# Gate products of u computed in the convolution stage, while u is on chip, and a merge stage without them

## The reference

```python
u = _rmsnorm(h, w['g_mix'][i])
proj = u @ w['w_in'][i]
...
xbc = silu(depthwise conv of width 3 over the tokens of xbc, plus conv_b)
...
gates = jax.nn.sigmoid(u @ w['w_gate'][i] + w['b_gate'][i])
g_a, g_s = jnp.split(gates, 2, axis=-1)
merged = g_a * (att @ w['w_att_up'][i]) + g_s * (ssm @ w['w_ssm_up'][i])
h = h + merged @ w['w_out'][i]
```

## Time and profile before

| | |
|---|---|
| three runs before | 3404.81, 3406.62, 3408.55 us, median 3406.62 |
| the profiled execution, its own time | 3404.74 us |
| its span, first to last instruction | 3403.2 us |
| TensorE busy | 2773.6 us, 81% |
| VectorE busy | 1692.1 us, 50% |
| ScalarE busy | 1264.1 us, 37% |
| GpSimd busy | 288.6 us, 8% |
| mean granted TensorE clock | 0.908 |

### The profile page before, as it was taken

One profiled execution on the slowest core, in us unless ns is written; L12 is line 12 of the kernel. 1 busy time (PEld: TensorE's weight loads), 2 busy tenths in 40 slices (PEclk: granted clock), 3 DMA queues, 4 the chain that ended last, 5 costly groups with the idle time before them and its releaser, 6 DMA issues. The chain is left out here.

```text
span 3403.2 us, 43260 instructions
## 1 busy us (share of the span) xinstructions
PE 2773.6 (81%) x15560; PEld 2377.3 (70%) x15560; DVE 1692.1 (50%) x2153; ACT 1264.1 (37%) x1737; POOL 288.6 (8%) x328
## 2 busy tenths in 40 slices
PE   3999999337754992698989695489999999999597
PEld 2898887236541771586868584489999999998475
DVE  5000000557877774333333224767777777777324
ACT  4111111346645554222222111055555555555222
POOL 0000000100020001000000000001111111110121
PEclk9999999578987995899999797589999999999799
DMA  8412211652113336546463562178787878785312
GB/s 263 111 62 93 81 63 56 183 156 61 33 55 88 103 108 187 175 123 197 127 194 93 169 195 74 33 228 258 235 258 235 260 235 257 240 258 168 115 39 97
DMA packets 477377, 507.50 MB, mean 149 GB/s; under 512 B 21096, under 2 KB 434664, under 8 KB 476424
## 3 DMA queue, kind: packets, MB, share of 16 engines
q1 hardware_dynamic: 444032, 375.44, 36.8%
q0 software_dynamic: 33264, 130.98, 12.1%
HBM read 397.12 MB, written 109.25 MB: 149 GB/s over the span
## 5 line engine op out<-in xcount | busy, mean ns | idle before, releaser
L1790 DVE TENSOR_TENSOR ex_w_lo<-ex_w_raw,ex_w_hi 128x2048 fp32r<-128x2048 f32 x195 | 443.8, 2291 | 142.9 <-ACT ex_w_hi L1747 142.9
L1879 PE MATMUL ex_ps_u<-ex_x,ex_w_hi 128*128 128x384 f32 x2048 | 411.5, 341 | 5.1 <-DVE ex_w_lo L1790 5.1
L1747 ACT ACTIVATE ex_w_hi<-ex_w_raw 128x2048 fp32r<-128x2048 f32 x195 | 370.5, 1909 | 0.8
L1879 PEld LDWEIGHTS ex_ps_u<-ex_x,ex_w_hi 128*128 128x128 f32 x2048 | 349.1, 189 | 6.2 <-issue 5.5
L1879 PEld LDWEIGHTS ex_ps_u<-ex_x,ex_w_lo 128*128 128x128 f32 x2048 | 265.6, 191 | 0.6
L1898 PE MATMUL ex_ps_d<-ex_w_hi,ex_h 128*128 128x512 f32 x768 | 265.8, 400 | 0.0
L1879 PE MATMUL ex_ps_u<-ex_x,ex_w_lo 128*128 128x192 f32 x2048 | 265.5, 272 | 0.0
L354 DVE TENSOR_TENSOR w_lo<-w_raw,w_hi 128x2048 fp32r<-128x2048 f32 x15 | 34.3, 2290 | 403.3 <-ACT w_hi L322 403.3
L328 ACT ACTIVATE stage<-ps 128x512 f32<-128x512 f32 (+1 forms) x102 | 55.8, 547 | 413.9 <-PE ps L376 358.4
L1898 PE MATMUL ex_ps_d<-ex_w_lo,ex_h 128*128 128x512 f32 x512 | 202.8, 396 | 0.0
L1898 PEld LDWEIGHTS ex_ps_d<-ex_w_hi,ex_h 128*128 128x128 f32 x768 | 144.6, 188 | 35.0
(11 more groups left out here) (366 smaller groups left out, 5219.4 us busy)
## 6 DMA issues: line engine op xcount, KB each, us to landing
ex_w_raw<-in_w_exp_gate SPq DMA_DIRECT2D x64, 1024.0 KB, 5.3
ex_w_raw<-in_w_exp_up SPq DMA_DIRECT2D x64, 1024.0 KB, 6.7
ex_w_raw<-in_w_exp_down SPq DMA_DIRECT2D x64, 1024.0 KB, 6.9
mg_w_raw<-in_w_gate SPq DMA_DIRECT2D x48, 512.0 KB, 5.2
w_raw<-in_w_in SPq DMA_DIRECT2D x15, 1024.0 KB, 5.6
mg_w_raw<-in_w_ssm_up SPq DMA_DIRECT2D x24, 512.0 KB, 6.1
xbcT_d<-stage POOLq DMA_DIRECT2D x5, 1536.0 KB, 5.6
cv_raw<-xbcT_d POOLq DMA_DIRECT2D x10, 768.0 KB, 5.6
```

Source lines behind the costliest of these rows:

```text
L1747: act.activation(w_hi[:, j % CUT], w_raw[:, j % RAW], ACT.Copy).then_inc(w_hi_done, 1)
L1790: dve.tensor_tensor(w_lo[:, j % CUT], w_raw[:, j % RAW], w_hi[:, j % CUT].bitcast(F32), ALU.subtract).then_inc(w_split, 1)
L1879: last = pe.matmul(ps_u[:, j % 2, m, 0:wide * C], w[:, s, k, cols], x[:, k, 0:wide].rearrange("p a c -> p (a c)"), start=i == 0, stop=i == ...
```

## The change

The 1152 gate matmuls (16 column tiles of w_gate by three blocks by 24) leave `merge_branches` and come into `convolve`, which now runs while u_hi and u_lo are still in SBUF. There they are 48 gate units, tile by tile. In each of the ten turns TensorE does one gate unit and then the turn's 12 transposes; 38 units follow behind the last turn. w_gate is loaded and split once (16 tiles of 128 x 1024), where the merge did it once for each block. ScalarE copies each gate product from PSUM (`gst`), SyncE stores it in DRAM (`g_d`).

`merge_branches` is written anew with 36 matmuls per unit: it loads the gate products from `g_d` (L1278 of the changed kernel), opens the gates ahead of the products, keeps o for all tokens in SBUF, holds y in two buffers and splits y of the next block a piece at a time between units (`TURNS`), and has four slots of PSUM for the products where it had two. In both stages the hardware loops (`Fori`) are gone: the instructions stand one behind the other. The core of the diff:

```diff
+    UNITS = [(i, col, blk) for i, col in enumerate(gate_tiles) for blk in range(NB)]
+    NG, NTL = len(UNITS), len(gate_tiles)
+    STEPS = max(XT, NG)
...
+            for n in range(XT):
+                if n >= 2:
+                    pool.wait_ge(mixed, n - 1)
+                pool.dma_start(raw[:, n % 2], xbcT_d[n]).then_inc(landed[n % 2], 16)
+                pool.dma_start(taps[:, n % 2], taps_d[n]).then_inc(landed[n % 2], 16)
...
+            conv(0)
+            split_lo(0)
+            for n in range(1, XT):
+                conv(n)
+                if n % NB == NB - 1:
+                    split_lo(n // NB + 1)
+            for t in range(XT // NB + 1, NTL):
+                split_lo(t)
...
+            def split_hi(t):
+                act.wait_ge(w_landed[t % 2], 16 * (t // 2 + 1))
+                if t >= 2:
+                    act.wait_ge(g_full, NB * (t - 1))
+                act.activation(w_hi[:, t % 2], w_raw[:, t % 2], ACT.Copy).then_inc(w_hi_done, 1)
...
+                if n < NG:
+                    act.wait_ge(g_full, n + 1)
+                    if n >= 2:
+                        act.wait_ge(g_out[s], 16 * (n // 2))
+                    act.activation(gst[:, s], ps_g[:, s], ACT.Copy).then_inc(g_copied, 1)
+                    if n % NB == 0 and n // NB + 1 < NTL:
+                        split_hi(n // NB + 1)
...
+            for n in range(STEPS):
+                s = n % 2
+                if n < NG:
+                    i, _, blk = UNITS[n]
+                    toks = slice(blk * BLK, (blk + 1) * BLK)
+                    pe.wait_ge(w_hi_done, i + 1)
+                    if n >= 2:
+                        pe.wait_ge(g_copied, n - 1)
+                    terms = [(w, u, k) for w, u in ((w_hi, u_hi), (w_hi, u_lo), (w_lo, u_hi)) for k in range(KT)]
+                    for j, (w, u, k) in enumerate(terms):
+                        if j == 2 * KT:
+                            pe.wait_ge(w_split, i + 1)
+                        last = pe.matmul(ps_g[:, s], w[:, i % 2, k], u[:, k, toks], start=j == 0, stop=j == len(terms) - 1)
+                    last.then_inc(g_full, 1)
+                if n < XT:
+                    pe.wait_ge(silu_done, n + 1)
+                    if n >= 2:
+                        pe.wait_ge(copied, n - 1)
...
+            def load_w(t):
+                if t >= 2:
+                    sp.wait_ge(w_split, t - 1)
+                col = gate_tiles[t] * P
+                sp.dma_start(w_raw[:, t % 2], w_view[:, :, col:col + P]).then_inc(w_landed[t % 2], 16)
+
+            for t in range(2):
+                load_w(t)
+            for n in range(STEPS):
+                s = n % 2
+                if n < NG:
+                    i, col, blk = UNITS[n]
+                    if blk == 0 and i + 2 < NTL:
+                        load_w(i + 2)
+                    sp.wait_ge(g_copied, n + 1)
+                    sp.dma_start(g_d[col // KT, col % KT, blk], gst[:, s]).then_inc(g_out[s], 16)
+                if n < XT:
+                    sp.wait_ge(copied, n + 1)
+                    sp.dma_start(xb_out[:, :, n * P:(n + 1) * P], nat[:, s]).then_inc(nat_out[s], 16)
...
-    parts = ((w_gate, 0, KT, "u"), (w_gate, D, KT, "u"), (w_att_up, 0, KO, "o"), (w_ssm_up, 0, KT, "y"))
-    KW = 3 * KT + KO
-    starts = (0, KT, 2 * KT, 2 * KT + KO)
+    KW = KO + KT
     M = D // P
+    UNITS = [(blk, tile) for blk in range(NB) for tile in range(M)]
+    NU = len(UNITS)
+    SLOTS = 4
+    TURNS = {2: (0, 1), 3: (2,), 4: (3,), 5: (4,), 6: (5,), 7: (6, 7)}
...
+            for n, (blk, tile) in enumerate(UNITS):
+                s = n % 2
+                cols = slice(tile * P, (tile + 1) * P)
+                if n >= 2:
+                    sp.wait_ge(w_split, n - 1)
+                for w, k0, k1 in ((w_att_up, 0, KO), (w_ssm_up, KO, KW)):
+                    sp.dma_start(w_raw[:, s, k0:k1], w.rearrange("(k p) c -> p k c", p=P)[:, :, cols]).then_inc(w_landed[s], 16)
+                if n >= 2:
+                    sp.wait_ge(gated, n - 1)
+                sp.dma_start(g_raw[:, s], g_d[:, tile, blk].rearrange("j p t -> p j t")).then_inc(g_landed[s], 16)
...
+            load_o(0)
             pool.wait_ge(newton, 4)
             load_y(0)
-            for blk in range(NB):
-                with pool.Fori(0, M // 2 - 1) as it:
-                    for s in range(2):
-                        store(blk, it, s, pool.snap(2 * it + s))
-                        seen_stored(blk, it, s)
-                store(blk, M // 2 - 1, 0, M - 2)
-                seen_stored(blk, M // 2 - 1, 0)
-                if blk < NB - 1:
-                    for name, hi_src, lo_src in sources:
-                        load(name, blk + 1, hi_src, lo_src)
+            for blk in range(1, NB):
+                load_o(blk)
+            for n, (blk, tile) in enumerate(UNITS):
+                s = n % 2
+                if tile == 0 and blk + 1 < NB:
+                    pool.wait_ge(y_lo_done, KT * (blk + 1))
                     load_y(blk + 1)
...
+            for n, (blk, tile) in enumerate(UNITS):
+                open_gates(n)
+                if n + 1 < NU:
+                    split_hi(n + 1)
+                if n:
+                    round_sum(n - 1)
+                if blk + 1 < NB:
+                    for k in TURNS.get(tile, ()):
+                        turn_y(blk + 1, k)
+            round_sum(NU - 1)
...
+            def combine(n):
+                s = n % 2
+                dve.wait_ge(full, n + 1)
+                dve.wait_ge(scaled, n + 1)
+                if n >= 2:
+                    dve.wait_ge(lo_done, n - 1)
+                for j in range(2):
+                    dve.tensor_tensor(prods[:, s, j], ps[:, n % SLOTS, j], gates[:, s, j], ALU.mult).then_inc(multiplied, 1)
+                dve.wait_ge(multiplied, 2 * n + 2)
+                dve.tensor_tensor(prods[:, s, 0], prods[:, s, 0], prods[:, s, 1], ALU.add).then_inc(summed, 1)
...
+                pe.wait_ge(w_hi_done, n + 1)
+                if n >= SLOTS:
+                    pe.wait_ge(multiplied, 2 * (n - SLOTS + 1))
+                if tile == 0:
+                    pe.wait_ge(o_landed[blk], 32)
+                terms = [(w, v, k) for w, v in ((w_hi, o_hi), (w_hi, o_lo), (w_lo, o_hi)) for k in range(KO)]
+                for i, (w, v, k) in enumerate(terms):
+                    if i == 2 * KO:
+                        pe.wait_ge(w_split, n + 1)
+                    pe.matmul(ps[:, n % SLOTS, 0], w[:, s, k], v[:, k, toks], start=i == 0, stop=i == len(terms) - 1)
+                terms = [(w, v, k) for w, v in ((w_hi, y_hi), (w_lo, y_hi), (w_hi, y_lo)) for k in range(KT)]
+                for i, (w, v, k) in enumerate(terms):
+                    if tile == 0 and i < KT:
+                        pe.wait_ge(y_hi_done, KT * blk + i + 1)
+                    if tile == 0 and i >= 2 * KT:
+                        pe.wait_ge(y_lo_done, KT * blk + i - 2 * KT + 1)
+                    last = pe.matmul(ps[:, n % SLOTS, 1], w[:, s, KO + k], v[:, blk % 2, k], start=i == 0, stop=i == len(terms) - 1)
+                last.then_inc(full, 1)
...
-    convolve(nc, tiles(xbcT), taps, ident, xb, bcT)
+        convolve(nc, u_hi_now, u_lo_now, w_gate, list(range(2 * KT)), tiles(xbcT), taps, ident, xb, bcT, g)
```

More of the change, by code:

```diff
@@ L1216, in _ @@
         @block.gpsimd
         def _(pool):
-            def load(name, blk, whole, half):
-                if blk:
-                    pool.wait_ge(used[name], blk)
-                for part, src, landed in zip(acts[name], (whole, half), a_landed[name]):
-                    pool.dma_start(part[:].bitcast(F32), src[:, :, blk * BLK:(blk + 1) * BLK]).then_inc(landed, 16)
-            def store(blk, it, s, tile):
-                n = it * 2 + (M * blk + s)
-                pool.wait_ge(lo_done, START + n + 1)
-                pool.sem_inc(pass_pool, 1)
-                for src, out in ((mh, m_hi_d), (ml, m_lo_d)):
-                    pool.dma_start(out[:, bass.ds(tile, 1), blk * BLK:(blk + 1) * BLK].rearrange("p o t -> p (o t)"), src[:, s].bitcast(F32)).then_inc(out_done[s], 16)
@@ new lines, in _ @@
+            for n, (blk, tile) in enumerate(UNITS):
+                s = n % 2
+                if tile == 0 and blk + 1 < NB:
+                    pool.wait_ge(y_lo_done, KT * (blk + 1))
+                    load_y(blk + 1)
+                pool.wait_ge(lo_done, n + 1)
+                for src, out in ((mh, m_hi_d), (ml, m_lo_d)):
+                    pool.dma_start(out[:, tile, blk * BLK:(blk + 1) * BLK], src[:, s].bitcast(F32)).then_inc(out_done[s], 16)
+            for done in out_done:
+                pool.wait_ge(done, 32 * NU // 2)
@@ new lines, in turn_y, with open_gates @@
+            def turn_y(blk, k):
+                act.wait_ge(y_landed, 16 * (blk + 1))
+                if blk >= 2:
+                    act.wait_ge(full, M * (blk - 1))
```

(43 more changed lines are left out.)

252 lines of the change are left out of this document (89 added, 163 removed).

## The result

| | before | after |
|---|---|---|
| median | 3405.72 us (3403.69 to 3408.55, 4 runs) | 3308.33 us (3306.51 to 3311.64, 4 runs) |
| ratio of after to before | | 0.9715, 95% interval 0.9698 to 0.9731 |
| span of the profiled execution | 3403.2 us | 3304.9 us |
| mean granted clock | 0.908 | 0.911 |

What follows compares the result with a forecast made beforehand. TensorE was taken to bound the merge and to be nearly free in the convolution. Merge -304.4 and convolution +216.4 give -88.0; 3404.74 - 88.0 + 1.9 = 3319 us, range 3303 to 3354 (the forecast's own 3308 to 3331).

Steps and rivals of the forecast that it cites:

- The frame: Whole change: 1152 matmuls move from the TensorE-bound merge to the convolution, where TensorE is nearly free; -304.4 and +216.4 us.
- Nine turns, 7.6 us each: Convolution, turns after the first: 7.6 us each from slower load landings, between 6.9 and 9.5; 68.4 us in all.
- 178 us under 188: Merge, steady units: 178 us of transfers hidden under 188 us of matmuls, the closest cover of the change.
- 38 units at 24 x 0.2266: Convolution, gate units behind the turns: 5.44 us each at the old merge's matmul pace, 206.7 us in all.
- Hidden, by 1 us: Convolution, first turn: low part of the weights ready at 616.0, before TensorE asks at 617.3, so no wait.
- End of the convolution, 7.7: Convolution, after the last gate unit: last copy 0.9 us, then store, landing and barrier 6.8 us.
- Merge's start, 43.8: Merge, stage start to end of first unit: 43.8 us, as that unit can't end before y arrives.
- Tail, 11.4: Merge, end of the stage: 13.4 us less a pair of sigmoids and one product done ahead, so 11.4 us.
- Block changes: Merge, between blocks: with o whole in SBUF and y split between units, the 38.6 us of losses go, except the cold start.
- Transfers as the limit, in turns or units: Two rivals, 12% each: transfers set convolution turns of 9.5 us (+17, 3336 us) or merge units of 9.5 us (+31, 3350).
- Waiting for the own stores: Rival, 3%: convolution gate units wait for their `gst` stores; at a landing of 15 us, +97, 3416 us.
- The clock: Rival, 4%: TensorE's clock stays low in the convolution's turns, making them 12.6 us; +45, 3364 us.

## Why the prediction was right, by its own steps

**The frame held.** Matmuls moved from a stage that TensorE bounds to one with TensorE nearly free; -304.4 + 216.4 was forecast and -308.9 + 212.8 came. That the total came out within 10 us is in part luck, as the next two steps show.

**Nine turns, 7.6 us each: mis-sized, 6.91.** The step is "a fuller queue makes landings longer: at 9 us it is 7.7". The rows have the loads of `cv_raw` landing in 5.5 us at a share of 0.88, no longer than the 6.4 of the earlier trace rows, and TensorE has no pause in the turns, so its own work is the turn: 24 x 0.2333 + 1.23 = 6.83. That the units there cost next to nothing was the mechanism, and the experiment with the units behind the turns shows it. The same step made too much of the transfers in the merge: 178 us under 188 were worked out with 277 and 322 GB/s. From 1600 to 1780 us in after the two queues moved 28.14 MB in 51.2% of 180 us and 15.40 MB in 21.8%, 305 and 392 GB/s while at work; the share was 0.72, not above 0.75, and even with double stores at 0.90 nothing waited. The 2 us of loss were 0.

**38 units at 24 x 0.2266: too low, 5.60.** The pace was taken from a stage whose weight tiles lie on multiples of 64 bytes, and these don't. This is 6.2 us of the sum, in the opposite direction to the turns; the two errors hid each other. The tile list of the change shows the odd start; nothing in the trace of before puts a price on it.

**"Hidden, by 1 us": wrong.** Counted from the stage's start, the low part was ready at 14.5 us, where 12.4 were forecast (616.0 - 603.64): the taps began 8.17 us in (611.21), not 6.15. TensorE asked at 11.6 us and not at 13.7: its first matmul came 1.2 us sooner, and it was at full pace after eight matmuls and not sixteen. That made 2.91 us of wait; the first turn was 1.5 us longer than forecast, and moving the split gave back those 1.5.

**End of the convolution, 7.7: 3.8.** It was read from the merge's end, where two stores follow one another on GpSimd's queue; here one store follows on SyncE's, 2.0 us to landing in the page's row for all 48:

```profile
g_d<-cv_gst SPq DMA_DIRECT2D x48, 256.0 KB, 2.0
```

**Merge's start, 43.8: 39.7.** The load of y took 9.05 us to its first rounding (10 forecast) but was issued 20.0 us into the stage, not 20.8, and the eight low-by-high matmuls at its end ran at full clock. **Tail, 11.4: 13.0.** From the last store's issue (1790.01) to the next stage are 8.6 us, where the earlier trace rows have 6.8; why that landing is slower wasn't tried.

**Block changes.** That the 35.6 us go (38.6 of losses less the 3.0 of the cold start) was right. The prediction put it down to o being whole and y being split between units; in this merge the runs say 30.3 for the late loads, y's early load among them, and 1.7 for the pieces of y.

**The rivals.** Transfers as the limit, in turns or units: the two rows at shares of 0.88 and 0.90 with TensorE busy throughout speak against both. Waiting for the own stores: `gst` is waited for by nobody, stores land in 2.0 to 3.4 us. The clock: 1.00 in the turns. The Trainium skill, TensorE: Matmul & The Clock Gate, Part 4, says that transposes don't count as busy for the clock. Where they stand alone (the units behind the turns) the clock is 0.55, and the trace agrees so far; but TensorE is idle for half of that stretch (25.5 of 56 us busy), which may be reason enough, and no run separates the two. Between gate units the transposes cost nothing, so the rule doesn't price this change.

## What to carry to other kernels

Work that an idle engine can take inside another stage's chain is nearly free until its own time per turn passes the chain's: here ten units of 5.6 us added 0.8 each. Behind that point every unit costs its full length, so the pace must be taken for the new place, with the tiles where they will lie: a 32-byte tile ahead of the weights cost 7 us, and moving it cost nothing. At a stage's start ask for what the first units need and hold the rest: an earlier first unit was worth nothing until the later loads (4.2 MB of o, and the variance) no longer stood beside the next weights. The moved tile, the first split ahead of the taps and the held start together give 3291.29 us, 17 below the changed kernel.

## What the runs showed of the hardware that wasn't expected

- fp32r matmuls of 128 x 128 by 128 x 512 at a clock of 1.00 take 0.2267 us with weight tiles at multiples of 64 bytes, and 0.2333 with tiles that begin 32 bytes past one; shown in two stages, in both directions. Whether it is the weights' high or low part, and what other offsets do, wasn't tried.
- Transfers at a share of 0.88 in the turns and 0.90 in the merge with double stores (270 and 307 GB/s) did not delay loads into double buffers enough for TensorE to wait.
- The clock rose to full speed at the end of the first eight gate matmuls (3.75 us for them, 2.13 for the next eight). In the pause for the low part behind them it sometimes fell again: in four runs whose convolution is that of the changed kernel the stage took 298.0 to 298.1 us and not 296.6, with matmuls or transposes at half clock behind the pause. Pauses of 2.58 and 2.91 us were without such a fall, pauses of 2.00 and of 3.09 to 3.25 with one. This is 1.4 us from one profiled execution to another that no edit caused, and what decides it stays open.
